# Scores of cached keys in a decode step: from transposes and one-column products on TensorE to products and sums on VectorE

## What is computed

```python
DILATED = ((128, 1), (512, 4), (2048, 16))      # window, stride
kg = ks[:, idx].astype(f32)                     # keys at distances 0, d, 2d, ... behind the query
logit = jnp.einsum('bqhd,bqjhd->bhqj', qf, kg) + bias[None, :, None, :]
...
p = jnp.exp(logit - m[..., None])
```

## Time and profile before

| what | value |
|---|---|
| median of 3 runs | 1557.72 us (1556.94 to 1562.88) |
| the profiled execution | 1562.38 us |
| its span, first to last instruction | 1560.6 us |
| PE busy / share | 1305.1 us, 84% |
| DVE busy / share | 350.6 us, 22% |
| ACT busy / share | 246.3 us, 16% |
| POOL busy / share | 73.8 us, 5% |
| mean granted TensorE clock | 0.927 of full |

### The profile page before, as it was taken

The page is one execution under the profiler, slowest core; times in us unless marked ns, Lnnn a source line. Parts: engine busy times, 40 slices in busy tenths (PEclk is TensorE's granted clock), DMA queues, the critical chain, the costliest instruction groups (busy, mean ns, idle before and its releaser), DMA issues.

```text
span 1560.6 us, 14815 instructions
## 1 busy us (share of the span) xinstructions
PE 1305.1 (84%) x5980; PEld 642.5 (41%) x5980; DVE 350.6 (22%) x793; ACT 246.3 (16%) x440; POOL 73.8 (5%) x81
## 2 busy tenths in 40 slices
PE   6989999999869887887887888869887888788775
PEld 3679876644453322232232234743322332233221
DVE  2064454432351100010010006460100010001006
ACT  3243543332110000000000003210000000000002
POOL 0000000000000000000000000000000000000000
PEclk9999999999969999999999999869999999889998
DMA  9344662524168999999999999118999999999993
GB/s 349 75 101 135 192 199 75 145 97 191 67 237 360 429 426 428 428 426 428 427 426 428 427 419 408 66 33 357 427 429 427 428 427 428 426 426 426 426 420 152
DMA packets 73163, 492.40 MB, mean 316 GB/s; under 512 B 15460, under 2 KB 21252, under 8 KB 48025
## 3 DMA queue, kind: packets, MB, share of 16 engines
q1 hardware_dynamic: 54784, 449.33, 69.9%
q0 software_dynamic: 12112, 31.96, 6.2%
q10 hardware_dynamic: 6225, 10.54, 2.0%
HBM read 479.73 MB, written 36.55 MB: 331 GB/s over the span
## 4 chain that ended last, share of the span: by engine, by line
PE 49%; DMA 40%; DVE 5%; ACT 2%; issue 2%; ACTq 0%; DVEq 0%
DMA ring<-in_moe_w 40%; PE ps L2102 15%; PE ps L1750 6%; PE ps L2112 6%; PE ps L1757 5%; PE ps L2037 3%; PE ps L2092 1%; PE ps L1799 1%; PE ps L1874 1%; PE ps L2140 1%; PE ps L1780 1%; PE ps L2275 1%; DVE arena L1262 1%; PE ps L1829 1%; PE ps L1806 1%
## 5 line engine op out<-in xcount | busy, mean ns | idle before, releaser
L2102 PE MATMUL ps<-ring,arena 128*64 128x512 f32 x2048 | 507.2, 653 | 138.5 <-DMA ring<-in_moe_w 134.9
L2102 PEld LDWEIGHTS ps<-ring,arena 128*64 128x64 f32 x2048 | 155.1, 150 | 486.6 <-issue 304.3
L2112 PE MATMUL ps<-ring,arena 128*64 128x512 f32 x1024 | 231.6, 605 | 26.6 <-issue 16.6
L1632 DVE TENSOR_TENSOR arena<-arena,ps 128x512 f32<-128x512 f32 x32 | 22.0, 687 | 821.2 <-ACT arena L1100 821.2
L2112 PEld LDWEIGHTS ps<-ring,arena 128*64 128x64 f32 x1024 | 85.6, 139 | 150.5 <-issue 139.6
L1750 PE MATMUL ps<-arena,ring 128*128 128x260 f32 x512 | 118.8, 391 | 0.9 <-ACT arena L837 0.9
L1100 ACT ACTIVATE arena<-ps 128x512 f32<-128x512 f32 x32 | 19.1, 597 | 573.2 <-PE ps L2102 573.2
L1750 PEld LDWEIGHTS ps<-arena,ring 128*128 128x128 f32 x512 | 98.2, 195 | 18.0 <-issue 1.7
L1757 PE MATMUL ps<-ring,arena 128*128 128x512 f32 x192 | 87.2, 601 | 0.0
L1106 ACT ACTIVATE arena<-ps,arena 128x1024 f32<-128x1024 f32 x32 | 35.6, 1113 | 315.0 <-PE ps L2112 315.0
L748 POOL DMA_INDIRECT arena<-hn_rows,arena x32 | 32.4, 1012 | 572.7 <-PE ps L2233 541.6
(11 more groups left out here) (278 smaller groups left out, 961.1 us busy)
## 6 DMA issues: line engine op xcount, KB each, us to landing
ring<-in_moe_w SPq DMA_DIRECT2D x96, 4096.0 KB, 22.2
ring<-in_w_in SPq DMA_DIRECT2D x7, 2048.0 KB, 19.6
y_rows<-c_zero POOLq DMA_DIRECT2D x2, 4160.0 KB, 18.9
ring<-y_rows SPq DMA_DIRECT2D x8, 1024.0 KB, 14.9
arena<-in_x_prompt SPq DMA_DIRECT2D x8, 512.0 KB, 6.2
ring<-in_w_out SPq DMA_DIRECT2D x2, 2048.0 KB, 10.8
hn_rows<-arena POOLq DMA_DIRECT2D x8, 512.0 KB, 3.1
arena<-i_rows SPq DMA_DIRECT2D x8, 256.0 KB, 7.3
```

The costliest lines, as they stand in the source:

```text
L2102: last = T.matmul(ps[r_, 2 + j, :], xgT[:, k, r_], w1v[:, slot, k, :], start=(k == 0), stop=(k == KC - 1))
L2112: last = T.matmul(ps[r_, 5 + c, :], hactT[:, k, r_], w2v[:, piece_slot(half, 2), k, c * 512:(c + 1) * 512], start=(k == 0), stop=(k == FC ...
```

## The change

The scores of the cached keys are made on DVE. The queries of the 8 samples are turned to rows by four PE transposes into bank 7 in step 35 (`QUERIES_AT`), copied by ACT in step 36 to SBUF and stored to a new buffer `q_rows` in memory (16 KB). POOL then broadcasts each sample's row of 512 to all 128 partitions (`qrep`, two buffers, 256 KB each); from the third on, a broadcast waits until the pair of tiles that used its buffer is scored. DVE's new `key_scores(q)`, at the end of `attended(s)` in the same steps as before, multiplies the key tile by the broadcast row and sums each head's 128 columns straight into `dscT`. The transposes, the copies by ACT, the one-column products, their semaphores and the copy of 64 columns are gone; the waits for them in `values`, `pick_samples` and `sample_logits` are dropped or replaced, SP waits for `key_scored` in place of `key_turned`, and a few pairs of semaphores are merged into one each (`brow_ready`, `snorm_ready`).

```diff
+        qrep = [at(11840 + 512 * i, AW) for i in range(2)]
+        kprod = [at(lo, AW) for lo in (13920, 14440)]
-        dscT = at(15169, 2, NB, HEADS)
+        dscT = at(19072, 2, NB, HEADS)
...
+        QUERIES_AT = 2 * UNIT[KA, 0] + 1
...
-            sp.wait_ge(key_turned, NB)
+            sp.wait_ge(key_scored, NB)
             output_weights(0)
...
-            sp.wait_ge(key_turned, 2 * NB)
+            sp.wait_ge(key_scored, 2 * NB)
             output_weights(1)
...
             pool.wait_ge(piece_done, upto(UNIT[KA, 0]))
             zeroed(y_rows[1], y_zeroed)
+
+            pool.wait_ge(q_stored, 16)
+            pool.wait_ge(ops_ready, 2)
+            for b in range(NB):
+                if b >= 2:
+                    pool.wait_ge(key_scored, 2 * (b - 1))
+                pool.dma_start(qrep[b % 2], q_rows[b:b + 1, :].partition_broadcast(P).rearrange("p a d -> p (a d)")).then_inc(qrep_in[b % 2], 16)
...
-            def key_columns(q):
-                act.wait_ge(key_turned, q + 1)
...
-                nc.scalar.activation(keyT[q % 2], ps[:, 7, :].rearrange("p (h k) -> p h k", h=HEADS), ACT.Copy).then_inc(keyT_ready, 1)
...
+                if s == QUERIES_AT + 1:
+                    act.wait_ge(sample_step, QUERIES)
+                    nc.scalar.activation(ib[0:NB, NT, :], ps[0:NB, 7, :], ACT.Copy).then_inc(q_out, 1)
+                    act.wait_ge(q_out, 1)
+                    act.dma_start(q_rows, ib[0:NB, NT, :]).then_inc(q_stored, 16)
...
+                if key_at(s) is not None:
+                    key_scores(key_at(s))
+
+            def key_scores(q):
+                b, t = q // 2, q % 2
+                if t == 0:
+                    dve.wait_ge(qrep_in[b % 2], 16 * (b // 2 + 1))
+                if q in (0, NB):
+                    dve.wait_ge(ring_in[KEY_SLOTS[q // NB]], CACHE_IN)
+                link(V.tensor_tensor(kprod[q % 2], kvv[:, KEY_SLOTS[q // NB], b % 4, t, :], qrep[b % 2], ALU.mult))
+                V.tensor_reduce(dscT[:, t, b, :], kprod[q % 2].rearrange("p (h k) -> p h k", h=HEADS), AX.X, ALU.add).then_inc(key_scored, 1)
...
-                    dve.wait_ge(dscore_done, 2 * NB)
-                    V.tensor_copy(dscT.rearrange("p t b h -> p (t b h)"), ps[:, 6, P:P + 64]).then_inc(decode_step, 1)
...
-                    pe.wait_ge(keyT_ready, 2 * NB)
+                    pe.wait_ge(q_out, 1)
...
-                if s > DECODE0:
-                    pe.wait_ge(decode_step, SCORES_OUT)
...
-            def turn_keys(q):
...
-            def key_scores(q, s):
...
+                if s == QUERIES_AT:
                     pe.wait_ge(piece_out, upto(UNIT[QA, HEADS - 1]))
...
+                    for h in range(HEADS):
+                        last = T.transpose(ps[0:NB, 7, h * DH:(h + 1) * DH], qT[:, h, SEQ:TOK], ident)
+                    last.then_inc(sample_step, 1)
...
-                pe.wait_ge(decode_step, SCORES_OUT)
+                pe.wait_ge(key_scored, 2 * NB)
```

More of the change, by code:

```diff
@@ L135, in build @@
     y_over = [nc.dram_tensor(f"y_over{l}", (2 * YROWS, D), F32, kind="Internal").ap() for l in range(2)]
+    q_rows = nc.dram_tensor("q_rows", (NB, AW), F32, kind="Internal").ap()
     i_rows = nc.dram_tensor("i_rows", (NB, AW), F32, kind="Internal").ap()
@@ L202, in build @@
         ivb = [at(24776 + 512 * i, AW) for i in range(4)]
-        keyT = [at(11840 + 512 * i, HEADS, P) for i in range(2)]
+        qrep = [at(11840 + 512 * i, AW) for i in range(2)]
+        kprod = [at(lo, AW) for lo in (13920, 14440)]
         ktok = [at(12864 + 512 * i, AW) for i in range(2)]
@@ L362, in build @@
         att_out = sem("att_out")
-        key_turned = sem("key_turned")
-        keyT_ready = sem("keyT_ready")
+        key_scored = sem("key_scored")
         kt_turned = sem("kt_turned")
@@ L368, in build @@
         ktok_stored = [sem(f"ktok_stored{i}") for i in range(2)]
-        dscore_done = sem("dscore_done")
+        q_stored = sem("q_stored")
+        q_out = sem("q_out")
+        qrep_in = [sem(f"qrep_in{i}") for i in range(2)]
         dprob_exp = sem("dprob_exp")
         decode_step = sem("decode_step")
-        SCORES_OUT, SELF_OUT, LOGITS_OUT, PROBS_OUT, PROBS_T_OUT, HEADS_OUT = 1, 2, 3, 4, 6, 8
+        SELF_OUT, LOGITS_OUT, PROBS_OUT, PROBS_T_OUT, HEADS_OUT = 1, 2, 3, 5, 7
         sample_step = sem("sample_step")
-        LOGITS, PROBS_TURNED, ATTENDED, GATES_TURNED, HEADS_TURNED = range(1, 6)
+        QUERIES, LOGITS, PROBS_TURNED, ATTENDED, GATES_TURNED, HEADS_TURNED = range(1, 7)
         lb_in = sem("lb_in")
@@ L405, in build @@
         s_read = sem("s_read")
-        osq_ready = sem("osq_ready")
+        snorm_ready = sem("snorm_ready")
         osq_summed = sem("osq_summed")
-        oms_ready = sem("oms_ready")
         oroot = sem("oroot")
@@ L620, in _ @@
             sp.wait_ge(i_stored, 16)
-            sp.wait_ge(dbias_ready, 1)
+            sp.wait_ge(brow_ready, 2)
             sp.wait_ge(bias_moved, 16)
@@ L949, in attend @@
                     exponentials(n)
-                q = key_at(s)
-                if q is not None:
-                    key_columns(q)
                 k = row_at(s)
@@ L991, in _ @@
                 if u == SAMPLE0 + 4:
-                    act.wait_ge(oms_ready, 1)
+                    act.wait_ge(snorm_ready, 2)
                     nc.scalar.activation(sroot, sms, ACT.Sqrt).then_inc(oroot, 1)
@@ L1190, in _ @@
             V.tensor_copy(brow[0:HEADS], ps[0:HEADS, 4:6, :].rearrange("p a b -> p (a b)")[:, 0:ROWW]).then_inc(brow_ready, 1)
-            V.tensor_copy(dbias[0:32], ps[0:32, 6, 0:NDEC]).then_inc(dbias_ready, 1)
+            V.tensor_copy(dbias[0:32], ps[0:32, 6, 0:NDEC]).then_inc(brow_ready, 1)
             dve.wait_ge(lb_exp, 1)
@@ L1814, in turn_probabilities @@
                 else:
-                    pe.wait_ge(oms_ready, 1)
+                    pe.wait_ge(snorm_ready, 2)
                 for j in range(i + 1):
@@ L1854, in turn_key_rows, with cached_keys @@
                 last.then_inc(kt_turned, 1)
-            def turn_keys(q):
[L1857 to L1863, removed]
-            def key_scores(q, s):
-                b, t = q // 2, q % 2
-                if q == 0:
-                    pe.wait_ge(piece_out, upto(UNIT[QA, HEADS - 1]))
[L1869 to L1885, removed]
+            def cached_keys(s):
+                if s == QUERIES_AT:
+                    pe.wait_ge(piece_out, upto(UNIT[QA, HEADS - 1]))
+                    for h in range(HEADS):
+                        last = T.transpose(ps[0:NB, 7, h * DH:(h + 1) * DH], qT[:, h, SEQ:TOK], ident)
+                    last.then_inc(sample_step, 1)
                 k = row_at(s)
@@ L1903, in sample_squares @@
             def sample_squares():
-                pe.wait_ge(osq_ready, 1)
+                pe.wait_ge(snorm_ready, 1)
                 T.matmul(ps[:, 5, 96:128], ones, osq.rearrange("p h b -> p (h b)"), start=True, stop=True).then_inc(osq_summed, 1)
@@ L1985, in _ @@
                         if c == IB:
-                            pe.wait_ge(dbias_ready, 1)
+                            pe.wait_ge(brow_ready, 2)
                         pick_samples(c)
@@ L1989, in _ @@
                     outputs(m - 1)
-                cached_scores(s)
                 attend(s)
@@ L2005, in _ @@
                     turn_decayed(m)
-                cached_scores(s + 1)
                 attend(s + 1)
```

9 lines of the change are left out of this document (2 added, 7 removed).

## The result

The changed kernel takes 1544.09 us (median of 5 runs, 1543.31 to 1548.49) against 1557.72 before: ratio 0.9912, 95% interval 0.9889 to 0.9935. That is 13.6 us or 0.9% faster, where 10.7 us and 1547.0 were forecast. The profiled execution took 1543.31 us, its span 1541.5.

A forecast was written before the change was run, and what follows sets the result against it. PE was taken to set the pace before 463 us, expert weights from 506.77 us on. 20.2 + 0.9 - 0.5 (query transposes) - 7.6 - 2.3 = 10.7 us off 1557.72 gave 1547.0 us, range 1536 to 1559.

The forecast's parts named there:

- PE before 463 us moves the end one for one: Layer 0's experts begin at 463.69 us behind PE work alone, so moving PE's earlier work moves the end equally.
- The first expert matmul: Sign of a right forecast: layer 0's expert matmuls, at 463.69 us before, would begin near 453.
- The removal, 20.2 us: On PE, 16 key tiles each lose 1.26 us of one-column products and transposes: 20.2 us off the path.
- the dip: PE's 0.85 us wait for ACT's copy at 267.21 and slow score instructions behind it; half counted, 0.9 us gained.
- DVE at nothing: DVE's added products and sums, 22.6 us for 16 tiles, fit under PE's units and cost nothing.
- rival 1: DVE becomes the bound; units one us longer than PE's cost 8, gain 2.7, 1555 us; chance 0.18.
- The stall, 7.6 us: PE waits from 189.7 to 197.3 for DVE's state step, behind the first query row landing at 195.0.
- The slow return, 2.3 us: After the stall PE runs slowly: 0.8 us on six level products, 1.5 on the next 16 projection matmuls.
- SP's second half of the keys and the broadcasts 2 to 7: Keys issued some 7 us later, broadcasts with about 12 us until needed: both hidden, costing nothing.
- Rival 2: Slow broadcasts make DVE wait before every pair of tiles; 1565 us at 15 us landing, 1591 at 19.3; chance 0.10.
- Rival 3: First broadcast slips in beside the fill, landing near 187; no stall or slow return, gain 20.6, 1537 us; chance 0.17.
- Units of about 9.7 us between 210 and 290: Sign of a right forecast: PE's projection units, some 12 us before, shrink to about 9.7 us there.

The follow-up runs named there:

- fill_after: Changed kernel with the zero fill of y_rows[1] put behind the eight query broadcasts on POOL's queue; 1536.5 us, ratio 0.9860.
- scores_later: Changed kernel with the first half of the cached keys scored half a unit later on DVE; 1543.2 us, ratio 0.9903.
- before_keys_first: Kernel before, with ACT's copy of the turned cached keys taken ahead of the rest of its half unit; 1558.0 us, ratio 1.0002.
- act_one_fill: Changed kernel with query rows 0 and 1 broadcast from ACT's queue, the other six from SP's, only fills on POOL's; 1548.2 us, ratio 0.9926.
- act_two_fills: As act_one_fill, with the fill of y_rows[0] held back to stand beside that of y_rows[1] on POOL's queue; 1550.9 us, ratio 0.9951.
- two_fills: Changed kernel with the fill of y_rows[0] held back, so both fills precede the first broadcast on POOL's queue; 1558.3 us, ratio 1.0003.
- product_twice: As fill_after, with DVE making each of the 16 key products twice; 1544.7 us, ratio 0.9914.

## Why the prediction was right, step by step

- **PE before 463 us moves the end one for one: right, as far as the medians can tell.** The stretch lost 13.96 us, the medians 13.6; with fill_after 23.05 and 21.6. Differences of a few us, as in scores_later and before_keys_first, they do not resolve. The first expert matmul came at 445.17, not near 453: the stretch gained 3.3 us more than forecast, and 4.6 of these two executions' difference lie outside it.
- **The removal, 20.2 us: right.** After minus before in the stretch is 20.2 + 2.6 (the dip) - 5.93 (the wait) - 2.90 and 0.18 (what ran slowly behind it) = 13.8, of 13.96 measured. The query transposes took 0.43 us, ahead of the stretch.
- **DVE at nothing: right, and shown.** Without the scoring the stretch is 0.13 us shorter, so rival 1 is out. It is not far away: half of the scoring once more already costs 2.94.
- **The stall, 7.6 us: the right place and the right chain, 1.7 us too long.** DVE waits for the row, then needs 2.42 us (forecast 2.35) until PE goes on. The row came 18.3 us after the fill's issue, where my numbers say 20.0 (174.96 to 195.0): a fill of 17.2 and some 1.1 behind it, against 18.0 and 2. (Two slips cancel in PE's side of the sum: 1.7 us of removed work stood between the fill's issue and 190.97, two tiles' transposes and one tile's products, not 1.26; and the 0.4 us of the query transposes were added to the fill's time and not to PE's.) The reason that I gave, the order on one queue, is only part of it: on a queue of its own the row is as late. What the step needed was "under the fill", not "behind the fill". The store of the queries, which I left out with "some 13 us to land", was slowed as well, 6.4 us from the end of its issue to POOL's release against 1.5 in fill_after; I take it as covered by the fill's own time, as I had said, since on POOL's queue the row comes behind the fill however early it is issued; no run made the store alone quicker.
- **The slow return, 2.3 us: 3.1 measured** (2.90 and 0.18). I took 0.8 on six level products and 1.5 on the block behind them; here the block came almost first and took nearly all of it. The length of the wait does not set it: the same block of 3.67 us took 6.57 behind 5.93 us and 5.86 behind 5.92 (act_one_fill), 5.30 behind 11.80 (act_two_fills) and 6.51 behind 19.21 (two_fills).
- **The dip, 0.9 us: mis-sized.** I took half of 0.85 + 0.85. Taking the wait away alone gives 2.60, since the low clock held to 272 and more rows than the two that I counted were slow. The short matmuls before it, which I thought might bring the fall by themselves, do not: the clock is 1.00 without the wait, here and in the changed kernel.
- **SP's second half of the keys and the broadcasts 2 to 7: hidden, right.** The keys were issued at 210.14, where the stretch began 3.0 us earlier than before: some 4 us late, not 7. The slowest of the eight broadcasts took 7.9 us, of 12 allowed. Rival 2 is out. The Trainium skill's fit in "DMA: Bandwidth & Descriptors", section "Anatomy of one DMA", gives 2.6 us by estimate for such a row; the quickest in the changed kernel took 3.2, the median 5.3, and these decide.
- **Rival 3, an early first broadcast, 1537: did not happen** in the changed kernel; its time is what fill_after reaches by taking the fill out of the way.
- **Units of about 9.7 us between 210 and 290: only at first.** From one turn of the decayed keys on PE to the next they took 9.5 and 9.9 us from 204.68 on, then 10.2 to 13.6: before, too, the five units behind the three shown took 11.81 to 16.21.

In sum the stall came 1.7 us shorter and the dip 1.7 larger than forecast, the return 0.8 slower: 10.7 + 1.7 + 1.7 - 0.8 = 13.3, against 13.6.

## What to carry to other kernels

When a step gets a new operand from DRAM, look for every large transfer that runs in the time before it is due, on whatever queue: moving the row to another queue gained nothing here with one fill ahead, moving the 4 MB fill, which had no due time of its own, gained 7.6 us. A wait of PE can cost more than its length, if the matmuls behind it run at the low clock: 0.85 us cost 2.6 in all and 5.93 cost 9.0, while 1.33 and 0.62 us in product_twice left the granted clock at 1.00. So read the clock behind each hole that a change closes or opens. And before an engine is called free, add work to it: DVE's 20 us cost nothing, 11 more already cost 3.

## What was not expected of the hardware

- A wait of 0.85 us ahead of a run of short matmuls cost 2.6 us in all in the kernel before (clock 0.87 over 13 us); one of 0.28 us at 256.80 in the changed kernel cost no clock (1.00 over the 13 us from 256).
- A 16 KB store on ACT's queue took 6.4 us under the fill, from the end of its issue to POOL's release, and 1.5 without it.
- The fill in pieces of 4 KB took 25.8 us at least, in pieces of 16 KB 17.2.
- Under one fill a row lands at the same time from the fill's own queue and from ACT's empty one (1.1 us after the fill); under two, the row from ACT's queue comes 8 us ahead of the second fill, and the row in the fills' queue 0.7 us behind it.
